# A hybrid decoder layer on one core: the second norm's last statistics issued inside the first up product

## The reference, cut to what matters

```
x = x + gt1 * mix
h = _rmsnorm(x, g2n) * (1 + sc2) + sh2
x = x + gt2 * (jnp.square(jax.nn.relu(h @ w_up)) @ w_down)
```

## Time and profile before

| what | value |
|---|---|
| median of 3 runs | 1805.4 us (1804.89 to 1807.15) |
| the profiled execution, own time | 1802.22 us |
| its span | 1800.4 us |
| TensorE busy | 1772.2 us, 98% |
| VectorE busy | 702.5 us, 39% |
| ScalarE busy | 487.0 us, 27% |
| GpSimd busy | 12.7 us, 1% |

### The profile page before, as it was taken

One profiled execution on the slowest core, in us unless ns is written; L12 is line 12 of the kernel. 1 busy time (PEld: TensorE's weight loads), 2 busy tenths in 40 slices (PEclk: granted clock), 3 DMA queues, 4 the chain that ended last, 5 costly groups with the idle time before them and its releaser, 6 DMA issues.

```text
span 1800.4 us, 26312 instructions
## 1 busy us (share of the span) xinstructions
PE 1772.2 (98%) x10976; PEld 1713.2 (95%) x10976; DVE 702.5 (39%) x1317; ACT 487.0 (27%) x832; POOL 12.7 (1%) x25
## 2 busy tenths in 40 slices
PE   8999999999999999999999989999999999999997
PEld 3899999999999999999999989999999999999997
DVE  3644324444544555333354563222222233434323
ACT  5443333223333233222232343222222211212111
POOL 0000000000000000000000020000000000000000
PEclk9999999999999999999999989999999999999999
DMA  9445544322331232211122111233233433323301
GB/s 311 144 136 157 177 129 131 83 58 73 88 92 55 65 100 58 59 47 47 49 84 84 47 36 47 59 95 91 89 92 90 137 95 95 95 93 97 93 34 65
DMA packets 215977, 165.33 MB, mean 92 GB/s; under 512 B 16091, under 2 KB 193159, under 8 KB 215926
## 3 DMA queue, kind: packets, MB, share of 16 engines
q1 hardware_dynamic: 209206, 155.97, 29.4%
q10 hardware_dynamic: 6720, 8.67, 1.4%
HBM read 133.83 MB, written 30.78 MB: 91 GB/s over the span
## 4 chain that ended last, share of the span: by engine, by line
PE 94%; DVE 2%; DMA 1%; issue 1%; ACT 1%; SPq 0%; DVEq 0%; ACTq 0%
PE PB L959 84%; PE M L887 3%; PE M L1012 1%; PE M L903 1%; DMA araw<-in_w_ada 1%; PE M L1087 1%; PE M L1093 1%; PE M L1079 1%; PE M L1081 1%; DVE XL L1257 1%; PE M L951 0%; PE M L1057 0%; DVE HB L1743 0%; DVE alo L1267 0%; ACT A L562 0%
## 5 line engine op out<-in xcount | busy, mean ns | idle before, releaser
L959 PE MATMUL PB<-XH,whi 128*128 128x352 f32 x2736 | 888.9, 325 | 4.1 <-DVE XL L1257 2.1
L959 PE MATMUL PB<-XH,wlo 128*128 128x352 f32 x2736 | 878.5, 321 | 0.0
L959 PE MATMUL PB<-XL,whi 128*128 128x352 f32 x2736 | 878.4, 321 | 0.0
L959 PEld LDWEIGHTS PB<-XH,whi 128*128 128x128 f32 x2736 | 514.0, 188 | 11.2 <-issue 6.9
L959 PEld LDWEIGHTS PB<-XL,whi 128*128 128x128 f32 x2736 | 515.3, 188 | 0.7
L959 PEld LDWEIGHTS PB<-XH,wlo 128*128 128x128 f32 x2736 | 513.8, 188 | 0.0
L580 ACT ACTIVATE whi<-raw 128x1024 fp32r<-128x1024 f32 x130 | 137.1, 1054 | 351.7 <-PE PB L959 348.2
L1262 DVE TENSOR_TENSOR wlo<-raw,whi 128x1024 fp32r<-128x1024 f32 x130 | 158.9, 1222 | 117.2 <-ACT whi L580 116.3
L1804 DVE TENSOR_TENSOR R<-R 128x1056 f32<-128x1056 f32 x32 | 40.3, 1259 | 271.5 <-ACT R L843 271.5
L1257 DVE SCALAR_TENSOR_TENSOR A<-PB,MOD,A 128x352 f32<-128x352 f32 (+1 forms) x96 | 54.9, 572 | 221.0 <-PE PB L959 221.0
L959 PE MATMUL PB<-AL,whi 128*128 128x352 f32 x384 | 123.9, 323 | 0.0
(11 more groups left out here) (301 smaller groups left out, 1293.0 us busy)
## 6 DMA issues: line engine op xcount, KB each, us to landing
raw<-in_w_in SPq DMA_DIRECT2D x64, 512.0 KB, 5.0
araw<-in_w_ada SPq DMA_DIRECT2D x48, 512.0 KB, 5.4
raw<-in_w_up SPq DMA_DIRECT2D x32, 512.0 KB, 4.8
raw<-in_w_down SPq DMA_DIRECT2D x32, 512.0 KB, 4.2
act_d<-R SPq DMA_DIRECT2D x24, 528.0 KB, 3.2
R<-act_d SPq DMA_DIRECT2D x24, 528.0 KB, 4.7
zp_d<-zr ACTq DMA_DIRECT2D x16, 512.0 KB, 2.7
Z<-zp_d SPq DMA_DIRECT2D x8, 1024.0 KB, 5.8
```

The source lines that it names most:

```text
L959: ins = pe.matmul(PB[:, bank, 0:BLK], w[:, w0:w0 + P], x[:, k, a0:a1], start=(k == 0 and j == 0), stop=(k == n_k - 1 and j == 2))
```

## The change

The column sums and the broadcast of third 2 leave their place between the last phase 4 product and the first up product. The sums are now issued inside the first up product, before its k tile 3 of third 0; the broadcast after that third's last k tile, before k tile 0 of third 1. On ScalarE the copy to `RSTD` of third 2 goes behind `h2_hi(1, 0)`. No instruction is added or removed, and the other queues read as before.

```diff
@@ ScalarE
         h2_hi(0, 6)
         h2_hi(0, 7)
-        rstd(2)
         for k in range(KT):
             h2_hi(1, k)
+            if k == 0:
+                rstd(2)
             if k == 3:
                 hi(T5_ + 1, 1)
@@ TensorE
         phase4(KT // 2 - 1)
-        rms_cols(2)
-        rstd_rows(2)
 
         def h2_ready(b, k):
+            if b == 0 and k == 3:
+                rms_cols(2)
+            if b == 1 and k == 0:
+                rstd_rows(2)
             if b == 2 and k == 0:
                 pe.wait_ge(s["hs_lo"], 1)
             pe.wait_ge(s["h2_lo"], KT * b + k + 1)
```

## The result

The changed kernel takes 1808.61 us (median of 18 runs, 1804.97 to 1811.87), the kernel before 1805.11 us (18 runs beside it, 1802.53 to 1807.15). The ratio is 1.0018, with a 95% interval of 1.0011 to 1.0025: 0.18% slower, 3.2 us with 2.0 to 4.5 as the interval (the two medians differ by 3.5).

The account below looks back on a forecast made before the run. VectorE, through its last low part, was taken to bound the stretch around the first up product. At half clock, 2.45 us late plus 0.26 overlap gave +2.7 on the 1805.4 median: 1808.1 us, range 1804.9 to 1811.0.

Parts of the forecast that it names:

- The second product's start is set by `h2_lo(2,7)`: End of the first up product: VectorE's last low part, not TensorE, sets when the second up product starts.
- the copy of third 2: ScalarE's copy behind the broadcast: starts at 1045.8 at half clock, against 1042.62 before, 3.2 us late.
- the high part of (1,1): ScalarE's h2_hi(1,1), queued behind the copy: ready at 1046.8 at half clock.
- VectorE's delay at the end: Last h2_lo: late by 2.45 + 0.26 = 2.7 us at half clock, with no slack to take it up.
- `h2_lo(1,1)` began 2.53 us later than before: VectorE waits for the high part of (1,1), so this tile begins 2.45 us later at half clock.
- its overlap with GpSimd: GpSimd's first tile of third 2 now overlaps h2_lo(1,1) on VectorE, adding 0.26 us.
- Half clock at the broadcast: TensorE's broadcast behind (0,7) runs at half clock after a thin stretch: +2.7 us, chance 0.53.
- bursts with waits between them: TensorE's third 0 becomes matmul bursts with waits of about 1 and 2.0 us, so the clock falls.
- the low clock stays: Rival: TensorE at low clock through third 2 into the second product, 4.8 to 6.8 us slower; chance 0.16.
- a wait of 1.27 us left the clock at full before: Argument against lasting low clock: TensorE's 1.27 us waits in thirds 1 and 2 left it at full.
- Full clock: Rival: the broadcast of third 2 runs at full clock, +1.5 us, 1806.9; chance 0.22.
- TensorE is the bound: Rival: third 0 moves into TensorE's idle time, end 5.9 us earlier, 1799.5; chance 0.03.

Follow-up runs that it names:

- the short low parts: Kernel before, with the low parts of third 2 made for 32 tokens in place of 320; stretch 24.52 us (before 25.75), ratio 0.9998.
- the two kernels in which TensorE works ahead for nothing: Changed kernel with the broadcast before (0,5), or straight behind the sums, and the copy ahead of h2_hi(1,0); ratios 1.0003 and 1.0001 to before.
- With the clock held up: Changed kernel plus 43 unused matmuls ahead of the waits of tiles (0,4) to (2,0); stretch 27.49 us, ratio 1.0011 to before.
- the scaling on ScalarE: Kernel before, with VectorE's scaling of feature tile 7 of third 2 moved to ScalarE; stretch 25.84 us, ratio 0.9996.
- without GpSimd: Kernel before, with all ten GpSimd scaling tiles given to VectorE; stretch 24.92 us, ratio 0.9993.
- the kernel without GpSimd in third 1: Kernel before, with GpSimd's five scaling tiles of third 1 given to VectorE; stretch 27.40 us, ratio 1.0001.

## Why the prediction was right, point by point

**What bounds the stretch.** "The second product's start is set by `h2_lo(2,7)`": shown by the short low parts, by the two kernels in which TensorE works ahead for nothing, and by the changed kernel itself, whose last `h2_lo` came 2.75 us later. It holds as long as TensorE is at full clock in third 2, or back at it soon enough; in five of the fourteen profiles it was not, and TensorE added 0.3 to 1.1 us of its own.

**The terms.** Counted from the last matmul of phase 4 and put on before's clock (minus 2.73 us), the copy of third 2 started at 1045.91 (1045.8 predicted), the high part of (1,1) was ready at 1046.86 (1046.8), and VectorE's delay at the end was 2.75 us (2.7). `h2_lo(1,1)` began 2.53 us later than before (2.45), and the other 0.22 us is its overlap with GpSimd (0.26); it took 0.81 us, where `h2_lo(1,0)` had taken 0.83 before. Half clock at the broadcast was the right one of the two. That the copy was met within 0.1 us has luck in it: the broadcast started 0.26 us later than reckoned, mostly because (0,5) and (0,6) ran at half clock too and TensorE came to (0,7) 0.17 us behind VectorE, and it took 1.46 us from its start to the copy's, where 1.63 was reckoned. With the clock held up the delay was 1.74, for which I had +1.5.

The Trainium skill, TensorE: Matmul & The Clock Gate, HAM oscillation, warned of bursts with waits between them. The trace agrees: the clock was at half from about the second wait (1.74 us, before (0,5)) until third 1. The waits in that section's case are for DMA and longer than these.

**What was left out of the sum.** I had the low clock leave no trace behind `h2_lo(2,7)`. It came back: TensorE recovered by 1050.5, fell again at about 1056.7 in the thin feed of third 1, and was at half clock until 1063.4, so that its tiles trailed VectorE's by 0.36 us at the end. This is the rival *the low clock stays*, in a small dose (it had 2.1 to 4.1 us); the clock was full again 2.2 us before the second product started. Against that rival I had set that a wait of 1.27 us left the clock at full before, and that was one execution: with the scaling on ScalarE, and TensorE's queue as before, a wait of 1.28 us was followed by half clock. How large the dose is seems to differ between executions: the mean clock of the 18 runs goes from 0.990 to 0.995, the slowest (1811.87 us) at 0.990, the three fastest (1804.97 to 1805.81) at 0.995. That this spread is the low clock in this stretch was not shown, since only one of them was profiled. The delay of VectorE and this tail give 3.11 us for a forecast of 2.7; the timed runs give 3.2.

**The rivals.** *Full clock*: no. *TensorE is the bound*: refuted by the stretches of 25.77 and 25.74 us. *No effect*: no; GpSimd's clashes did not go away with a late start, they only moved.

## What to carry to other kernels

An engine's idle time is only worth filling if it is the one that sets the end: here TensorE's waits were full of VectorE's work, and filling them gained nothing. When a producing step is moved behind a tile, ask what that tile waits for, and what stands in the same queue behind the consumer of the step: tiles (1,1) to (1,7) needed nothing from third 2 and were held up only by standing behind its copy. And two engines that slow each other are one resource: work given from VectorE to GpSimd at 0.4 us a tile came back as about 0.6 us a tile of waiting. That is an estimate: without GpSimd VectorE made ten tiles more, some 4.2 us, waited 1.19 us for the roots and still had its last `h2_lo` 0.79 us earlier, 6.2 us over ten tiles. And the nine matmuls ahead of the sums, worthless with GpSimd at work, came with a stretch 0.8 us shorter without it.

## What the runs showed of the hardware that I had not expected

- While GpSimd multiplies two SBUF operands tile after tile, most of VectorE's SBUF instructions take about as long as a GpSimd tile, small or large: a 128x32 one took 0.85 us (0.18 without GpSimd), 128x352 ones 1.19 to 1.30 us (0.51 to 0.58 alone), beside GpSimd tiles of 1.01 to 1.13 us. A few get through at their own time, like the 0.51 us at 1037.27 in before. The Trainium skill, SBUF — State Buffer, Who interferes with whom, says the loser is blocked until the other's instruction ends; the starts 1.11 to 1.12 us apart in the kernel without GpSimd in third 1 (1042.65, 1043.77, 1044.88), beside GpSimd tiles of 1.13, agree.
- So taking one VectorE instruction out of such a stretch gains little, 0.2 us of its 0.98; the next one takes its place in the wait.
- Fillers that nobody reads held the granted clock at 1.00 through a stretch that was at 0.68 to 0.75 without them, and the one execution profiled with them was about 1.4 us shorter in this stretch, though TensorE had 43 more matmuls to do.
- The same wait does not always bring the same clock. Behind 1.69 us of idle time the sums ran at half clock in before and at full with the scaling on ScalarE; at the start of third 2 it was the other way round, behind 1.27 and 1.28 us.
